# Recurrence's tail moved into the compression, loads reordered, and the routing rebuilt, in a one-core decoder layer

## The chip, the cores and the metric

One of the eight cores of a Trainium2 chip runs the whole kernel. The metric is the device time of one execution in microseconds (us); less is better. Engines: PE (TensorE, matrix products; PEld is its weight load), DVE (VectorE), ACT (ScalarE), POOL (GpSimd), SP (SyncE, which here only issues DMAs). They run side by side and are ordered by semaphores alone.

## The reference, cut to what matters

One layer for a prompt of 256 tokens and 8 samples of one token, which share all weights (264 token columns in all):

```python
h = rms_norm(x)                               # D_MODEL 1024
p = h @ w_in                                  # RWKV-7 columns, NSA columns, two merge gates
y_a = rwkv7(p_a)                              # 8 heads of 64: S = S*w + (S a) b^T + v k^T ; y = S r
                                              # then group norm, bonus, gate
y_b = nsa(p_b)                                # compressed, selected and windowed attention over paged caches
x = x + (sig(g_a) * (y_a @ w_br_a) + sig(g_b) * (y_b @ w_br_b)) @ w_out
h = rms_norm(x)                               # norm_ffn
logits = h @ w_router + b_router              # 32 experts, top 4, softmax over the 4
x = x + sum_k w_k * (swiglu(h @ w_up[e] + b_up[e]) @ w_down[e] + b_down[e])
y = rms_norm(x)
```

The compressed branch of the attention passes each block of 32 cached rows (keys and values apart) through a two-layer network with a gelu, for the samples' 1024 past positions and the prompt's own rows.

## The kernel before, in words

Everything is fp32. The work is a row of blocks; in each, every engine has its own hand-written list of instructions, and a block ends when all engines are through with theirs. A helper `step` (line 132) makes an instruction signal its engine and the engine wait for it; `copy` on ACT has one line in a block.

- **Projection** (`project`, 203): norm, the input projection, and the inputs of the recurrence.
- **Recurrence** (`rwkv_chunks`, 533): the prompt's 256 tokens in chunks of 64. PE, ACT and DVE invert the chunks' triangular matrices in five levels (`t1`, `dxy`; DVE masks the next level at line 675). Beside it POOL advances the 8 samples' states in products of 128x2048 (lines 650 to 658), with two sums on DVE (710, 731); the state goes out, and the samples' y goes through DRAM to be turned by PE (873). The block's tail is the group norm of y: means and variances by PE (879, 882), squares and roots on ACT, reciprocal, product and affine on DVE (739 to 741), bonus and gate on POOL (662, 663). SP also loads the compression's early weights here, and POOL gathers piece 0 of the cache.
- **Compression** (`compress`, 911): 64 units. In unit u PE turns two tiles of gathered rows (1081), ACT (u even) or DVE (u odd) copies them to one of four buffers, and PE multiplies those of unit u-2 with the first layer's weights (1045). Pieces of 1 MB serve 8 units each; three buffers hold them, so piece p is gathered once unit 8(p-2) is turned (`cmp_piece`, 168). At nine units a set-up product uses bank 3 (`at_unit`, `setup`, 1048): three for the table of relative biases (1056), four of the queries, the gates, and 16 small ones for the compressed scores' biases (1069). SP issues page ids, `hot`, the late weights, and then `rel_bias`, which the first set-up waits for along with `hot`.
- **Prompt's attention** (`attend_prompt`, 1102): compressed scores, their softmax on DVE and ACT, turned at line 1100 and copied at 1202; between them PE makes the first merge-gate tiles (1252), whose weights SP loads at the block's start (1130), two buffers deep. Then 16 units of scores (1277), exp, turns and values, with a gate tile in each of the first twelve. POOL issues 16 gathers of selected rows (1147) at the start and the copy of the window cache (1149).
- **Samples' attention** (1319) and **merge** (1559), which at its end adds to x, loaded again.
- **Routing** (`route`, 1651): SP loads six constants (1693), then expert 0's up and down weights, and stores h for the gathers. POOL loads the experts' biases three times over; ACT and DVE split them into three bf16 parts (1719, 1751, 1808), stacked in 96 rows. The norm of x waits for the constants (1749); PE turns h (1828) with ACT's evictions, multiplies with the router (1833). DVE adds the bias (1756), finds the top four, and from ranks by PE (1839, 1841) derives for each token its slot in its expert's 64-row tile; lines 1776 to 1784 list the experts of overflow tiles. PE turns the cells into a table of rows (1846), which DVE reads at 1811. The weights' normalisation ends DVE's list (1817, 1818).
- **Experts** (`first_tiles`): 32 experts. SP streams 8 MB of up and 4 MB of down weights per expert through 16 slots of a ring; a slot is refilled once PE has used it (`up_used`, `down_used`). POOL gathers an expert's rows of h and scatters its results. PE: up products (2016), up bias by a one-hot `pick` in bf16 (2022), turns (1997, 2003), down products (2034), down bias (2039). Overflow tiles (`further_tiles`) aren't run with these inputs.
- **Finish**: the four results of a token are added, and the last norm.

## Time and profile before

| what | us |
|---|---|
| median of 3 runs (lowest, highest) | 1717.59 (1707.12, 1718.58) |
| the profiled execution | 1712.36 |
| its span in the profile | 1710.6 |
| PE busy in the span | 1355.0 (79%) |
| DVE, ACT, POOL busy | 371.0, 223.0, 171.6 |

The profiled execution's time holds its span and 1.8 us around it. "Granted clock" is the share of TensorE's full clock (2.4 GHz) that it was given, 0.50 being the lower level of 1.2 GHz. A releaser (`<-`) behind an idle time is the instruction or DMA that the profile names as the one that ended it. DMA share is the mean busy share of the core's 16 DMA engines.

### The profile page before, as it was taken

The numbers are of one execution on the slowest core, as the hardware profiler recorded it, in microseconds if no ns is written. First come the engines' busy times: TensorE is split into PE (matmuls) and PEld (weight loads), VectorE is DVE, ScalarE is ACT, GpSimd is POOL, SyncE is SP. The second block draws the span as 40 slices with busy tenths as digits, with TensorE's granted clock in tenths as the row PEclk, the third lists the DMA queues.
The fourth block names the chain that finished last, engine by engine and source line by source line (L and its number), as shares of the span: only waits on it lengthen the run. The fifth ranks groups of instructions, "written<-read, shape, count | busy, mean of one in ns | idle before, by whom it ended". The sixth has DMA issues, their size and how long they took to land. (4 is left out here: it accounts for less than half of the span.)

```text
span 1710.6 us, 21148 instructions
## 1 busy us (share of the span) xinstructions
PE 1355.0 (79%) x8102; PEld 690.3 (40%) x8103; DVE 371.0 (22%) x792; ACT 223.0 (13%) x478; POOL 171.6 (10%) x226
## 2 busy tenths in 40 slices
PE   6998838997998945797788887777887887778870
PEld 5878724665877834232222222222222222222220
DVE  3457441122335215111001001010010010100104
ACT  2211120221222023010000000000000000000001
POOL 1004520121000000100000000100001000000010
PEclk9999965898989985799999999999999999999995
DMA  5425133237214446899999999999999999999953
GB/s 173 130 62 120 27 89 106 75 121 297 90 70 129 124 116 254 338 416 415 418 417 415 418 416 417 418 415 418 416 417 418 415 418 416 415 418 415 416 237 141
DMA packets 142944, 489.60 MB, mean 286 GB/s; under 512 B 18958, under 2 KB 67344, under 8 KB 109440
## 3 DMA queue, kind: packets, MB, share of 16 engines
q1 hardware_dynamic: 131848, 457.15, 68.6%
q0 software_dynamic: 10640, 31.11, 5.1%
q8 instruction: 41, 0.67, 0.2%
q10 hardware_dynamic: 400, 0.55, 0.1%
q14 instruction: 15, 0.12, 0.0%
HBM read 484.37 MB, written 16.95 MB: 293 GB/s over the span
## 5 line engine op out<-in xcount | busy, mean ns | idle before, releaser
L2016 PE MATMUL bank<-ex_ring,ex_work 128*64 128x512 f32 x2048 | 515.6, 634 | 170.1 <-DMA ex_ring<-in_w_up 168.3
L2016 PEld LDWEIGHTS bank<-ex_ring,ex_work 128*64 128x64 f32 x2048 | 136.2, 142 | 521.3 <-DMA ex_ring<-in_w_up 299.1
L2034 PE MATMUL bank<-ex_ring,ex_work 128*64 128x512 f32 x1024 | 226.8, 595 | 0.8 <-ACT ex_work L1938 0.8
L1973 DVE TENSOR_SCALAR ex_work<-bank 128x512 f32<-128x512 f32 x32 | 22.1, 692 | 713.6 <-PE bank L2022 713.6
L2034 PEld LDWEIGHTS bank<-ex_ring,ex_work 128*64 128x64 f32 x1024 | 70.7, 137 | 134.1 <-issue 133.1
L1918 POOL DMA_INDIRECT scratch_choice<-ex_work,ex_di x32 | 33.4, 1043 | 665.6 <-ACT ex_work L1948 665.6
L468 PE MATMUL bank<-hT,w_group 128*128 128x264 f32 (+1 forms) x400 | 92.6, 394 | 0.6 <-DVE hT L371 0.6
L468 PEld LDWEIGHTS bank<-hT,w_group 128*128 128x128 f32 (+1 forms) x400 | 76.0, 191 | 16.1 <-issue 0.7
L1252 PE MATMUL bank<-hT,w_cmp 128*128 128x264 f32 x256 | 66.2, 408 | 4.7 <-DMA w_cmp<-in_w_in 4.7
L1938 ACT ACTIVATE ex_work<-bank 128x512 f32<-128x512 f32 x32 | 19.1, 597 | 359.3 <-PE bank L2003 359.3
L1934 ACT ACTIVATE ex_work<-bank 128x512 f32<-128x512 f32 x33 | 19.7, 598 | 344.2 <-PE bank L1997 344.2
L1252 PEld LDWEIGHTS bank<-hT,w_cmp 128*128 128x128 f32 x256 | 49.1, 200 | 15.6 <-DMA w_cmp<-in_w_in 5.2
L1948 ACT ACTIVATE ex_work<-bank 128x512 f32<-128x512 f32 x32 | 19.1, 597 | 202.2 <-PE bank L2039 202.2
L1984 DVE COPY ex_pick_down<-ex_pick 96x64 bf16 x31 | 5.9, 191 | 158.6 <-PE bank L2039 158.6
L1910 POOL DMA_INDIRECT ex_work<-scratch_h,ex_si x33 | 34.6, 1048 | 41.1 <-POOL ex_si L1905 24.3
L1010 DVE COPY pT<-bank 128x256 f32<-128x256 f32 x32 | 13.6, 426 | 101.2 <-PE bank L1081 100.9
L1997 PE MATMUL bank<-masks,ex_work 128*128 128x128 f32 x132 | 22.1, 291 | 12.2 <-DMA ex_work<-scratch_h,ex_si 12.2
L1081 PE MATMUL bank<-masks,x 128*128 128x128 f32 x96 | 18.6, 326 | 14.6 <-PEq L120 14.6
L1618 PE MATMUL bank<-mixed,sel_rows 128*128 128x264 f32 x128 | 28.7, 387 | 1.5 <-DVE mixed L1592 1.5
L1045 PE MATMUL bank<-pT,w_cmp 64*128 64x265 f32 x128 | 29.9, 553 | 0.0
L1618 PEld LDWEIGHTS bank<-mixed,sel_rows 128*128 128x128 f32 x128 | 24.2, 190 | 6.0 <-DVE mixed L1592 1.9
L1905 POOL COPY ex_si<-src_row 128x1 uint32 (+1 forms) x33 | 6.1, 185 | 190.2 <-DMA scratch_choice<-ex_work,ex_di 182.0
(465 smaller groups left out, 1370.1 us busy)
## 6 DMA issues: line engine op xcount, KB each, us to landing
ex_ring<-in_w_up SPq DMA_DIRECT2D x256, 1024.0 KB, 17.9
ex_ring<-in_w_down SPq DMA_DIRECT2D x256, 512.0 KB, 17.2
w_group<-in_w_in SPq DMA_DIRECT2D x12, 1024.0 KB
w_cmp<-in_w_in SPq DMA_DIRECT2D x8, 1024.0 KB, 7.4
sel_rows<-in_w_out SPq DMA_DIRECT2D x8, 512.0 KB, 7.2
choice_rows<-scratch_choice SPq DMA_DIRECT2D x2, 2048.0 KB, 10.4
out_win_s<-in_state_win_kv POOLq DMA_DIRECT2D x1, 4088.0 KB, 26.8
win_rows<-in_state_win_kv SPq DMA_DIRECT2D x6, 512.0 KB
```

The costliest lines, as they stand in the source:

```text
L468: mm = mmul(banks[2 + i % 4][0:n, 0:T], w[:, g % 3, kc, c:c + n], hT[:, kc, :], start=(kc == 0), stop=(kc == KD - 1))
L1045: mmul(banks[4 + 2 * kv + g][:, 0:T + 1], w1[r // 16][gs, kv, r % 16, :], fl[gs, u % 4, :], start=(r == 0), stop=(r == 31)).then_inc(hid, 1)
L1252: mm = mmul(gate_bank(t)[:, 0:T], w[:, t // 2 % 2, kc, P * (t % 2):P * (t % 2) + P], C["hT"][:, kc, :], start=(kc == 0), stop=(kc == KD - 1))
L1618: mm = mmul(banks[m % 2][:, 0:T], sel[:, c, m // 4, m % 4, P:256], mix[:, c, :], start=(c == 0), stop=(c == KD - 1))
L1910: pool.indirect_dma_start(B["xg"][:], None, halves(scratch["h"]), bass.IndirectOffsetOnAxis(ap=B["si"][:, 0:1], axis=0), bounds_check=last ...
L1918: pool.indirect_dma_start(halves(scratch["choice"]), bass.IndirectOffsetOnAxis(ap=B["di"][:, 0:1], axis=0), B["y"][:], None, bounds_check= ...
L1934: nc.scalar.activation(B["xT"][:].rearrange("p a b -> p (a b)"), banks[6][:], ACT.Copy).then_inc(S["xT_ready"], 1)
L1938: nc.scalar.activation(B["hT"][:].rearrange("p a b -> p (a b)"), banks[7][:], ACT.Copy).then_inc(S["hT_ready"], 1)
L1973: nc.vector.tensor_scalar(g[:], banks[0][:], 7.0, None, ALU.min).then_inc(S["g_ready"], 1)
L1997: mm = nc.tensor.transpose(banks[6][:, P * k:P * k + P], B["xg"][:, P * k:P * k + P], ident)
L2016: mm = mmul(banks[n // 2][lo:lo + SLOTS, :], B["xT"][:, k % 4, SLOTS * (k // 4):SLOTS * (k // 4) + SLOTS], B["ring"][:, k, 512 * n:512 * n ...
L2034: mm = mmul(banks[4][SLOTS * n:SLOTS * n + SLOTS, :], B["hT"][:, k % 4, SLOTS * (k // 4):SLOTS * (k // 4) + SLOTS], B["ring"][:, 8 + 4 * h ...
```

## The change

- The samples' part of the recurrence and the whole group norm leave the recurrence's block and become part of the compression. The samples' state is advanced by DVE in 16 tasks of 128x1024 (`sample_half`), one in each odd unit below 32. Eight more set-up products (means and variances) and the turn of the samples' y are placed at units 38 to 56; ACT takes squares and roots, DVE the reciprocals at units 55 to 61, POOL bonus and gate as the norms come. The final state's stores are waited for in the compression.
- The compression has eight piece buffers (in the room of the selected rows), and POOL issues all seven gathers at its start. `rel_bias` is loaded ahead of the late weights. The 16 small bias products go. After unit 31 SP loads the first two groups of gate weights.
- The prompt's attention reads the compressed scores' biases from the bias table in four additions, after a memset by POOL. POOL waits for a gate tile before each pair of gathers of selected rows, and for the twelfth before the window copy.
- Samples' attention: two of the window buffers lie in x. Merge: SP loads the routing's six constants after x.
- Routing: PE turns x itself; DVE evicts with the norm's gain, and the root of the mean square is applied to the logits. The biases are loaded once, in fp32 (32 rows), with no split; the bias products of the experts are fp32. SP loads up weights of expert 0, stores h, then loads the down weights of experts 0 and 1. The list of overflow experts is made by fewer operations behind the comparison (`hit`), which is cut into three parts with a signal each; the weights' normalisation stands ahead of the table's wait.

The diff, cut to its core:

```diff
@@ cmp_piece, gate_weights
-                pool.indirect_dma_start(C["raw"][p % 3][:, t, :], None, src, ...)
+                pool.indirect_dma_start(C["raw"][p][:, t, :], None, src, ...)
+        def gate_weights(sp, g):
+            c0 = 3096 + 256 * g
+            sp.dma_start(C["gate_w"][:, g % 2], a["w_in"][0][:, c0:c0 + 256]...).then_inc(C["gate_in"][g % 2], 16)
@@ rwkv_chunks
-                    tt_(tmp[:], sS[:], keys(kk), ALU.mult).then_inc(prod, 1)
-                    step(tt_(sS[:], sS[:], keys(w), ALU.mult))
...
-                    for m in range(4):
-                        mmul(banks[m][:, 0:T], mean_m, y[:, m, :], start=True, stop=True).then_inc(mean_d, 1)
...
-                    sp.wait_ge(wkv_out, 64)
@@ compress
-                at_unit = [6 + 4 * i for i in range(9)]
-                on_act = (3, 4, 5, 6, 7)
+                at_unit = [4, 8, 12, 16, 18, 20, 22, 26, 38, 40, 42, 44, 46, 50, 52, 54, 56]
+                on_act = (3, 4, 5, 6, 7, 8, 13, 14, 15, 16)
                     sp.dma_start(hot, a["c_hot"]).then_inc(hin, 16)
+                    sp.dma_start(rel[:], a["rel_bias"]).then_inc(hin, 16)
                     cmp_weights(sp, w1[1], 1, w_late)
-                    sp.dma_start(rel[:], a["rel_bias"]).then_inc(hin, 16)
...
+                    sp.wait_ge(hid, 64)
+                    for g in range(2):
+                        gate_weights(sp, g)
...
-                    cmp_piece(pool, 1)
-                    cmp_piece(pool, 2)
-                    for p in range(3, 8):
-                        pool.wait_ge(turned, 8 * (p - 2))
+                    for p in range(1, 8):
                         cmp_piece(pool, p)
...
+                        if u < 32:
+                            if u == 1:
+                                dve.wait_ge(s_in, 16 * 14)
+                            sample_half(u // 2)
+                        if u in (55, 57, 59, 61):
+                            m = (u - 55) // 2
+                            dve.wait_ge(set_a, n_a(14 + m))
+                            step(nc.vector.reciprocal(e[:, m, :], e[:, m, :]))
@@ attend_prompt
-                    for g in range(NG // 2):
-                        if g >= 2:
-                            sp.wait_ge(mtd, 2 * (g - 1))
+                    for g in range(2, NG // 2):
+                        sp.wait_ge(mtd, 2 * (g - 1))
+                        gate_weights(sp, g)
...
                     for s in range(NB):
+                        pool.wait_ge(mtd, s + 1)
...
+                    pool.wait_ge(mtd, 12)
                     pool.dma_start(o["win_s"]...)
@@ route, SP
+                    sp.dma_start(B["bias"][:, 0:2 * FF], a["b_up"][0]).then_inc(b_in, 16)
...
-                    for k in range(8):
-                        sp.dma_start(B["ring"][:, 8 + k // 2, ...], a["w_down"][0][0, P * k:P * k + P, :])...
                     for t, (t0, n) in enumerate(TILES):
                         sp.wait_ge(hg_ok, t + 1)
                         sp.dma_start(scratch["h"][t0:t0 + n, :], h[0:n, t, :]).then_inc(st_, 16)
+                    for e in range(2):
+                        for k in range(8):
+                            sp.dma_start(B["ring"][:, 8 + 4 * e + k // 2, ...], a["w_down"][0][e, P * k:P * k + P, :])...
@@ route, DVE and PE
+                    for k in range(KD):
+                        dve.wait_ge(hTd, k + 1)
+                        ts_(hT[:, k, :], banks[k % 2][:, 0:T], col("norm_ffn", k), None, ALU.mult).then_inc(hTe, 1)
...
-                        step(tt_(lg[0:n, t, :], banks[2 + t][0:n, 0:NEXP], br[0:n, :], ALU.add))
+                        step(stt(lg[0:n, t, :], banks[2 + t][0:n, 0:NEXP], ss[0:n, t:t + 1], br[0:n, :], ALU.mult, ALU.add))
...
-                    pe.wait_ge(hg_ok, 3)
                     for k in range(KD):
...
-                            mm = nc.tensor.transpose(banks[k % 2][:, t0:t0 + n], h[0:n, t, P * k:P * k + P], ident[0:n, 0:n])
+                            mm = nc.tensor.transpose(banks[k % 2][:, t0:t0 + n], x[0:n, t, P * k:P * k + P], ident[0:n, 0:n])
@@ expert_buffers
-            for name, shape, dt in (("ring", [P, 16, 2 * FF], F32), ("bias", [96, 3 * FF], BF16), ("pick", [96, NEXP + 1], BF16),
+            for name, shape, dt in (("ring", [P, 16, 2 * FF], F32), ("bias", [NEXP, 3 * FF], F32), ("pick", [NEXP, NEXP + 1], F32),
```

## Rows read from the trace of the kernel before

**Rows 1.** Windows by stage; columns as in the first line.

```profile
core 0: us, PE busy (x) PEld busy (x) DVE busy (x) ACT busy (x) POOL busy (x), PEclk, DMA share, GB/s
...
150.00:195.00 45.00, 34.97 (x931) 32.93 (x928) 34.17 (x37) 6.46 (x11) 34.59 (x11) 0.89 0.35 74
...
213.30:241.10 27.80, 6.70 (x21) 5.07 (x21) 14.37 (x19) 5.70 (x13) 5.92 (x8) 0.65 0.03 6
...
249.80:262.50 12.70, 0.76 (x6) 0.32 (x6) 0.00 (x0) 0.48 (x2) 0.00 (x0) 0.60 0.99 218
262.50:296.00 33.50, 33.50 (x106) 17.73 (x106) 4.77 (x16) 2.90 (x12) 3.76 (x4) 0.50 0.27 86
296.00:370.00 74.00, 71.76 (x433) 46.72 (x432) 13.20 (x53) 16.69 (x57) 5.65 (x7) 0.93 0.17 55
370.00:405.80 35.80, 26.54 (x129) 21.22 (x129) 6.34 (x20) 2.77 (x5) 19.07 (x34) 0.76 0.95 367
...
622.70:686.40 63.70, 23.85 (x114) 19.82 (x114) 30.83 (x77) 23.95 (x31) 3.49 (x7) 0.51 0.70 249
...
697.10:1665.00 967.90, 797.18 (x3520) 244.98 (x3520) 94.61 (x191) 74.87 (x129) 78.03 (x126) 0.97 1.00 408
```

**Rows 2.** Timeline, recurrence, DVE's masking line and POOL's first product: start, us, instruction.

```profile
147.15 0.69 DVE L675 TENSOR_TENSOR m_level_wu<-m_L,masks 128x512 f32<-128x512 f32 x1
...
153.17 4.56 POOL L650 TENSOR_TENSOR rw_bt_kt<-sample_state,sample_vec 128x2048 f32<-128x2048 f32 x1
...
154.06 4.23 DVE L675 TENSOR_TENSOR m_level_wu<-m_L,masks 128x512 f32<-128x512 f32 x1
```

**Rows 3.** Timeline, end of the recurrence and start of the compression.

```profile
212.60 0.68 PE L869 MATMUL bank<-masks,m_AK 64*64 64x64 f32 x16
...
238.60 0.74 POOL L663 TENSOR_TENSOR yaT<-pT,rw_gate 128x264 f32<-128x264 f32 x1
...
241.10 2.90 PE L1081 MATMUL bank<-masks,x 128*128 128x128 f32 x12 [14.55 <-PEq L120]
```

**Rows 4.** Timeline, compression, PE: bias table and layer-one products.

```profile
262.49 1.87 PE L1056 MATMUL bank<-yb_tok,rel_bias 32*8 32x512 f32 x2 [11.95 <-DMA rel_bias<-in_rel_bias]
...
267.77 1.25 PE L1045 MATMUL bank<-pT,w_cmp 64*128 64x265 f32 x4
...
270.10 1.25 PE L1045 MATMUL bank<-pT,w_cmp 64*128 64x265 f32 x4
...
305.39 0.72 PE L1045 MATMUL bank<-pT,w_cmp 64*128 64x265 f32 x4
...
306.68 0.72 PE L1045 MATMUL bank<-pT,w_cmp 64*128 64x265 f32 x4
```

**Rows 5.** Timeline, start of the prompt's attention, PE.

```profile
398.01 3.58 PE L1100 MATMUL bank<-masks,cmp_p 128*8 128x128 f32 x16 [8.06 <-DVE cmp_pT L1202]
...
405.79 1.57 PE L1277 MATMUL bank<-pT 64*128 64x128 f32 x8
```

**Rows 6.** Timeline, routing, to expert 0's first products.

```profile
641.16 6.63 PE L1828 MATMUL bank<-masks,ex_work 128*128 128x128 f32 x24 [20.41 <-DVE ex_work L1749]
...
648.27 7.99 PE L1833 MATMUL bank<-w_router_sb,h_T 128*128 128x32 f32 x48 [0.48 <-ACT h_T L1725]
...
656.37 0.18 DVE L1756 TENSOR_TENSOR logits<-bank,b_router_sb 8x32 f32<-8x32 f32 x1 [0.24 <-PE bank L1833]
...
665.21 0.68 DVE L1779 TENSOR_TENSOR over_w<-extra_base,numbers 1x512 f32<-1x512 f32 x1
...
675.93 1.76 DVE L1805 TENSOR_TENSOR h_T<-numbers,rt_slot 128x1536 f32<-128x1536 f32 x1
...
697.10 8.26 PE L2016 MATMUL bank<-ex_ring,ex_work 128*64 128x512 f32 x24 [0.69 <-ACT ex_work L1934]
```

**Rows 7.** Timeline, an expert's last K step of up and its biases.

```profile
1025.63 1.94 PE L2016 MATMUL bank<-ex_ring,ex_work 128*64 128x512 f32 x8 [0.57 <-DMA ex_ring<-in_w_up]
...
1027.40 0.60 PE L2022 MATMUL bank<-ex_bias,ex_pick_up 96*64 96x512 bf16 x4
```

More of the change, by code:

```diff
@@ L146, in build @@
         prm = sb(ctx, "prm", [P, NPRM])
+        gain = sb(ctx, "ffn_gain", [P, D])
+        R = {}
+        after = P
+        for name, cols_ in (("wr", KD * NEXP), ("num", 2 * P + 1), ("rk", 2 * P), ("br", NEXP), ("dest", 3 * TOPK * 2)):
+            R[name] = masks[:, after:after + cols_]
+            after += cols_
+        R["wr"], R["rk"] = R["wr"].rearrange("p (c n) -> p c n", n=NEXP), R["rk"].rearrange("p (c n) -> p c n", n=P)
+        R["dest"] = R["dest"].rearrange("p (t k j) -> p t k j", t=3, k=TOPK)
+        R["in"] = sem("route_consts_in", True)
         x = sb(ctx, "x", [P, 3, D])
@@ L191, in rwkv @@
                 ar = sb(st, "rw_at_rt", [P, 2, 4, T])
-                q = {n: sb(st, "rw_" + n, [P, 4, T]) for n in ("gate", "k2")}
+                q = {"gate": C["gate"], "k2": sb(st, "rw_k2", [P, 4, T])}
                 bk = sb(st, "rw_bt_kt", [P, 2, 4, T])
@@ L619, in _ @@
                     act.wait_ge(yd, 1)
-                    copy(y[:, :, P:TP].rearrange("p m (c t) -> p c m t", c=2), banks[5].rearrange("p (c m t) -> p c m t", c=2, m=4)).then_inc(ye, 1)
-                    for m in range(4):
-                        act.wait_ge(cent, m + 1)
-                        nc.scalar.activation(e[:, m, :], y[:, m, :], ACT.Square).then_inc(sqr, 1)
-                    act.wait_ge(eps_ok, 1)
-                    for m in range(4):
-                        act.wait_ge(var_d, m + 1)
-                        nc.scalar.activation(e[:, m, :], banks[4 + m][:, 0:T], ACT.Sqrt, bias=eps[:, 0:1]).then_inc(root, 1)
+                    copy(y[:, :, P:TP].rearrange("p m (c t) -> p c m t", c=2), banks[5].rearrange("p (c m t) -> p c m t", c=2, m=4))
                 @block.gpsimd
@@ L982, in _ @@
                                 nc.scalar.activation(qg[:, i - 3, :], banks[3][:, 0:T], ACT.Copy, scale=SCALE).then_inc(set_a, 1)
+                            elif i == 8:
+                                copy(y[:, :, TP:T], banks[3][:, 0:4 * TS].rearrange("p (m t) -> p m t", m=4)).then_inc(set_a, 1)
+                            elif i >= 13:
+                                act.wait_ge(eps_ok, 1)
+                                nc.scalar.activation(e[:, i - 13, :], banks[3][:, 0:T], ACT.Sqrt, bias=eps[:, 0:1]).then_inc(set_a, 1)
                             else:
@@ L1563, in merge @@
                 oT = sb(st, "outT", [P, KD, T])
-                ta, tb = sb(st, "gated_a", [P, 2, T]), sb(st, "gated_b", [P, 2, T])
+                ta, tb = (C["gate"][:, 2 * i:2 * i + 2, :] for i in range(2))
                 ab, mix_ok, od, oe, td, te = (sem("mg_" + n) for n in
@@ L1733, in _ @@
                                              accum_out=tsum[0:n, t:t + 1]).then_inc(ex, 1)
-                    act.wait_ge(rest_ok, 2)
-                    copy(B["bias"][64:96], rest[64:96])
                 @block.vector
@@ L1762, in _ @@
                     red(asg[:], oh[:].rearrange("p t k e -> p t e k"), axis=AX).then_inc(asg_ok, 1)
+                    for j in range(2):
+                        step(tt_(cell[:, :, :, j, 0:NEXP], oh[:], dest[:, :, :, j].unsqueeze(3).to_broadcast([P, 3, TOPK, NEXP]), ALU.mult))
                     dve.wait_ge(rkd, 1)
```

315 lines of the change are left out of this document (147 added, 168 removed).

## The prediction

> **What bounds the kernel now.** I cut the span into stages with the view by windows [rows 1], then read, stage by stage, the timeline for what the next stage's first instruction had waited for.
>
> The last 1000 us are the 32 experts. From 697.1 to 1665 us the DMA moves 408 GB/s at a share of 1.00, while PE is busy 797 of 968 us [rows 1]: the weights' transfer sets this stage, and PE idles 171/32 = 5.3 us per expert. A product in the stage waits for its weights by half a microsecond at a time [rows 7]. So nothing before the stage helps by making it faster; an edit helps by letting its first product come earlier than 697.10 [rows 6].
>
> In the first 700 us no one engine is full. PE is the busiest, and what is lost lies in places where it stands: 6.7 busy of 27.8 us at the recurrence's end, 0.8 of 12.7 us early in the compression, then 33.5 us of full work at a granted clock of 0.50, 26.5 of 35.8 us at the start of the prompt's attention, 23.9 of 63.7 us in the routing [rows 1]. The change touches each of these.
>
> **Part A, samples' state taken out of the recurrence (150 to 195 us).** POOL's 128x2048 products go. Beside the first, of 4.56 us, DVE's 128x512 masking took 4.23 us; the same line took 0.69 us before POOL began [rows 2]. PE idles 45.0 - 35.0 = 10.0 us in the stretch, with the granted clock at 0.89 [rows 1]. These DVE operations feed the next product of the chain, so most of the idle time is theirs. What stays is the true chain product, copy, product. Bounds: 3 us (only the three worst meetings), 14 us (all idle time and the low clock). I take 9, nearest to the idle time.
>
> **Part B, the recurrence's tail.** PE's last product of the recurrence proper starts at 212.60 and takes 0.68; PE next has steady work at 241.10, 27.8 us on. The last instruction of the tail (POOL, 238.60 + 0.74) ends 1.8 us before that, which is the price of the change of block [rows 3]. Afterwards only the copies of the final state and of y and SP's two stores stand between: by a 128x512 operation of 0.69 us [rows 2] and two DMA issues about 2 us, and 1.8 us for the change: 3.8 us. The final waits for these stores go with the block's last lines. Gain 24; bounds 20 and 26.
>
> **Part C, the compression (241.1 to 370.0 us, 128.9 us).** A unit is one pair of turned rows plus a layer-one product. At full clock units follow each other by 306.68 - 305.39 = 1.29 us, at half clock by 270.10 - 267.77 = 2.33 us [rows 4]. Built up for the changed kernel:
> - 64 units at 1.29 = 82.6 us.
> - 17 set-up products. The bias row took 1.87 us at the low clock [rows 4], 0.95 at the full one; three of these, four head products, eight means and variances (each about as a layer-one product, 0.5 to 0.7 us) and two small ones: 10.6 us. The old kernel's 16 tiny bias products go.
> - the ends: the first turns, then gelu, keys and values as a chain of some ten operations of 0.5 to 0.7 us, which I put at 7 us, as before.
> That is 100 us. Three additions:
> - PE's stall of 11.95 us on the bias table goes [rows 4]: its DMA is now issued ahead of the late weights, and not behind them. I leave 1 to 2 us, since seven gathers of 1 MB are now issued at once (7 MB at 408 GB/s [rows 1] is 17 us, and the 2 MB of late weights beside them). Piece p is needed after 8p units, 10.3p us, so the flood keeps ahead of its readers.
> - DVE gets 16 tasks of 128x1024 in the odd units up to 31. From 0.69 us for 512 columns [rows 2] a task is about 1.3 us, one of them in each half 2.5. DVE's own copies are some 0.6 us of a two-unit period of 2.58, so 1.9 of 2.58 is full, and a copy has more than 1 us of slack because three banks are in use. Cover is there at both clocks. At the end the four reciprocal, product, affine chains (some 2.7 us each beside a copy) come every 2.58 us: that falls behind by 0.7 each and costs PE 2 us.
> - The low clock. 33.5 us at 0.50 followed the stall of 12.7 us [rows 1]. Without the stall I expect shorter stretches, about 18 us in all: 9 us more. Bounds: none, and the whole 44 us as before (20 us).
> The Trainium skill ("TensorE: Matmul & The Clock Gate", section "What's actually happening") has the array back at full clock after a short stretch of sustained work. The row of 262.5 to 296 us disagrees: PE was busy all 33.5 us and the granted clock stayed at 0.50. By the page's rule this stage would end some 9 us earlier than I say; I go by the row.
> Sum 112 us, gain 17; bounds 0 (all of the low clock returns, with flood stalls) and 27.
>
> **Part D, the prompt's attention up to its first scores (370.0 to 405.8 us, 35.8 us).** The gate weights' first two loads move into the compression, and the 16 gathers of the selected rows wait for one gate product each. Now the DMA is saturated here (share 0.95, 367 GB/s [rows 1]), PE stands for 8.06 us before the second turning of the compressed probabilities, and the first scores come at 405.79 [rows 5]. In all PE idles 35.8 - 26.5 = 9.3 us with a granted clock of 0.76 [rows 1]. With gate weights at hand and the DMA not full, about 1 us of the idle time stays and 2 us of the low clock goes: 26 us. The bias is now added in four operations in place of eight, with cover under the gates. Queued behind POOL's new waits is only its own window copy, which lands long before 504 us. That copy now starts after the twelfth gate and meets the last gate load: 0 to 3 us. Gain 10; bounds 0 and 12.
>
> The samples' attention changes only places of buffers: nothing. The merge gains six DMAs on SP, behind the loads that PE waits for and none ahead of them: nothing, since the merge's own products cover them. Without that cover they would cost the routing what they cost now.
>
> **Part E, routing (622.7 to 697.1 us).** Two things hold the first turn until 641.16: the wait for the constants' DMAs and the norm's products behind it (PE's 20.41 us of waiting [rows 6]). Afterwards x is turned at once, at 622.8. Eight turns with an eviction each, 6.6 us as now [rows 6], end at 629.4; the 48 router products, 7.99 us, at 637.4. Meanwhile DVE does the norm's three 128x1024 products (from rows 2 about 4 us) after its last eviction and is free at 634.5. So the last logit addition, now at 656.37, comes at 637.5: 18.9 us. From there to the table: five of the over-list's operations of 0.68 and two or three small ones leave the path (4.0 us), one 0.6 us product goes, 0.2 is added: 4.4 us. The 1.76 us comparison goes in three parts, and PE begins after the first: 1.2 us. The weights' normalisation (six small operations of 0.2, as the one at 656.37) leaves the tail: 1.3 us. Sum 25.8 us, so routing ends near 661 in place of 686.4 and expert 0's first product stands near 671, the gather's 10.7 us (686.4 to 697.10 [rows 1, 6]) kept. The bias parts on ACT and DVE go altogether. Bounds 18 and 29 (with the array at full clock right behind the merge, where the row has 0.51).
> Who is late next: SP now issues 8.4 MB of up and 8.4 MB of down weights, at 408 GB/s done near 666. That is before 671, but the first gather's rows travel with them, as they do now; and expert 1's down weights, which now are loaded in this gap, are no longer to be loaded there.
>
> **Part F, biases in fp32.** The four bias products of up took 0.60 us in bf16; one K step of the same shape in fp32 takes 1.94 [rows 7]. So +1.3 for up, +0.6 for down, 1.9 us per expert against 5.3 idle: hidden for 31 experts. Past the last transfer nothing hides it: two down biases and one up bias, +2.5 us. Upper bound per expert: about 6 us, if the products don't pair.
>
> **Sum.** 9 + 24 + 17 + 10 + 25.8 - 2.5 = 83.3 us. Against the profiled execution, 1712.36 us (its span 1710.6): 1629. The median of the runs is 1717.59, 5.2 above it, so I predict 1634.
>
> **Rivals.**
> 1. The compression stays at half clock although it isn't stalled. For: the row 262.5 to 296. Against: 296 to 370 us, the same work, has 0.93 [rows 1]. Price: in 40 us of low clock 18 us in place of 9, 1643; for all 64 units 64 x 1.04 = 67, less 9: 1692.
> 2. The flood: gathers, late weights and DVE's tasks stall the compression as the saturated DMA does in part D, by 8 to 20 us: 1642 to 1654. For: 8.06 us of stall under 367 GB/s [rows 5]. Against: work waits here for 1 MB per 10 us only.
> 3. Routing's end falls to SP's queue or to the first gather behind 17 MB of weights: 5 to 8 us late, 1641.
> 4. The other side: PE overtakes the DMA as the experts' bound. One mechanism: 1.9 us more per expert at a long low clock. At full clock it has room (24.9 + 1.9 against 30.2 us). At half clock an expert takes 53.6 against 30.2, 23 us lost for each. It decides once four experts in a row run so: 83/23. Eight would give 1634 + 187 = 1821. Against: clock 0.97 over the stage [rows 1], and more work on PE doesn't call for a lower one.
> 5. More than forecast: full clock in the compression and the routing, 1615.
>
> **How the numbers follow.** Forecast 0.58, rival 1 0.12, rival 2 0.12, rival 3 0.07, rival 4 0.03, rival 5 0.08. Predicted is the likeliest, 1634. The range 1610 to 1668 takes in rivals 2, 3 and 5, and rival 1 but for its worst. A measurement of this kernel can tell about 1%, 17 us. Faster by over 1%: 0.95; within: 0.02; slower: 0.03 (rival 4).
>
> **What would show each step.** In the changed profile: DVE's masking line at 0.69 us throughout (A); some 4 us from the recurrence's last product to the compression's first (B); no wait on the bias table, a stage of about 112 us and its granted clock (C); 26 us to the first scores (D); from the merge's end to the first expert product about 49 us where there were 74 (E); the experts' stage again near 968 us at 408 GB/s (F). If that stage is longer by more than 10 us, or the compression over 125 us, the prediction is wrong.

## Result and profile after

| | before | changed |
|---|---|---|
| median of 4 runs (lowest, highest), us | 1718.09 (1707.12, 1720.77) | 1628.15 (1623.85, 1631.19) |
| profiled execution (span), us | 1712.36 (1710.6) | 1623.85 (1622.0) |
| PE busy, mean granted clock of the experts' stage | 1355.0, 0.97 | 1371.4, 1.00 |

The changed kernel takes 0.953 of the time of before [0.948, 0.957], 5% less. Forecast were 1634 us and a range of 1610 to 1668. Profile against profile 88.5 us are gained; the sum of the forecast was 83.3. Executions of one kernel fall into two states some per cent apart, and every ratio in this document compares fast executions with fast ones, so it can differ from the ratio of two medians.

The view by windows, cut at the first instructions of the same stages as in [rows 1]; columns as there:

```profile
core 0: us, PE busy (x) PEld busy (x) DVE busy (x) ACT busy (x) POOL busy (x), PEclk, DMA share, GB/s
150.00:204.45 54.45, 47.78 (x1401) 45.64 (x1401) 27.07 (x48) 8.68 (x14) 3.16 (x4) 1.00 0.20 43
204.45:208.71 4.26, 0.68 (x17) 0.57 (x17) 0.80 (x3) 1.04 (x3) 0.00 (x0) 0.97 0.20 35
208.71:309.86 101.15, 96.19 (x574) 61.01 (x574) 54.66 (x120) 27.27 (x89) 22.44 (x23) 0.96 0.49 144
309.86:336.77 26.91, 26.91 (x128) 22.46 (x129) 5.76 (x16) 2.77 (x5) 9.19 (x24) 0.79 0.45 153
336.77:437.52 100.75, 92.37 (x482) 78.15 (x481) 35.24 (x112) 27.16 (x93) 10.10 (x11) 0.91 0.43 154
...
551.96:603.36 51.40, 25.41 (x127) 20.72 (x127) 29.33 (x89) 7.73 (x18) 2.01 (x4) 0.55 0.91 358
603.36:1573.10 969.74, 843.55 (x3712) 247.55 (x3712) 94.03 (x191) 74.62 (x128) 77.87 (x126) 1.00 0.99 407
1573.10:1622.00 48.90, 0.04 (x2) 0.00 (x0) 19.68 (x21) 5.71 (x11) 0.99 (x1) 0.54 0.35 126
```

The timeline of the changed kernel at those places (start, us, instruction, idle time before it and its releaser):

```profile
154.37 0.69 DVE L644 TENSOR_TENSOR m_level_wu<-m_L,masks 128x512 f32<-128x512 f32 x1
...
204.45 0.68 PE L825 MATMUL bank<-masks,m_AK 64*64 64x64 f32 x16
208.71 2.90 PE L1102 MATMUL bank<-masks,x 128*128 128x128 f32 x12 [3.58 <-PEq L120]
...
215.50 1.02 PE L1073 MATMUL bank<-yb_tok,rel_bias 32*8 32x512 f32 x2
...
309.86 6.14 PE L1268 MATMUL bank<-KcT,pT 64*128 64x8 f32 x32 [1.01 <-PEq L857]
...
336.77 1.57 PE L1302 MATMUL bank<-pT 64*128 64x128 f32 x8
...
405.32 3.89 PE L1277 MATMUL bank<-hT,w_cmp 128*128 128x264 f32 x8 [4.47 <-DMA w_cmp<-in_w_in]
...
561.74 7.99 PE L1829 MATMUL bank<-masks,h_T 128*128 128x32 f32 x48 [0.59 <-DVE h_T L1745]
...
603.36 3.68 PE L2012 MATMUL bank<-ex_ring,ex_work 128*64 128x512 f32 x8 [0.69 <-ACT ex_work L1930]
...
1553.23 1.93 PE L2018 MATMUL bank<-ex_bias,ex_pick_up 32*64 32x512 f32 x8
```

Read against the rows of before:

| stretch | before | changed | gain | forecast |
|---|---|---|---|---|
| A: to the recurrence's last product (L869, now L825) | 212.60 | 204.45 | 8.2 | 9 |
| B: from there to the compression's first turn | 28.50 | 4.26 | 24.2 | 24 |
| C: compression, to the attention's first product | 128.92 | 101.15 | 27.8 | 17 |
| D: from there to the first scores | 35.77 | 26.91 | 8.9 | 10 |
| first scores to samples' attention | 98.73 | 100.75 | -2.0 | 0 to -3 |
| samples' attention and merge, to its last product | 115.04 | 114.44 | 0.6 | 0 |
| E: merge's last product to expert 0's first | 77.54 | 51.40 | 26.1 | 25.8 |
| F: experts' stage | 967.6 | 969.8 | -2.2 | 0 |
| F: last product to the end | 45.9 | 48.9 | -3.0 | -2.5 (both F rows) |

Four of the rows come out within 1 us. The one large gap is C, and most of it is the clock: PE turns its first pair at 208.71, meets the bias table at 215.50 without a wait, and from 217 us up to the end of the 64 units, near 299 us, the granted clock is 1.00, where before had 33.5 us at 0.50 [rows 1, 4]. The gap is 10.8 us; 9 of it is the low clock that the forecast kept, the rest the small waits that it allowed for and that did not come. The experts' stage moves 407 GB/s, as before; the bias products (L2018, 1.93 us) stand where PE would have waited.

### The profile page after: what moved, and what is told of

Read it like the earlier page. It is cut to its first block and busy times, and to the rows that moved or that the text cites. A ratio compares the mean times of both kernels' runs of the same rounds, so it can differ in the third digit from the quotient of the medians.

```text
span 1622.0 us, 21473 instructions
## 1 busy us (share of the span) xinstructions
PE 1371.4 (85%) x8262; PEld 674.8 (42%) x8263; DVE 372.4 (23%) x810; ACT 206.1 (13%) x464; POOL 139.5 (9%) x213
## 5 line engine op out<-in xcount | busy, mean ns | idle before, releaser
L2012 PE MATMUL bank<-ex_ring,ex_work 128*64 128x512 f32 x2048 | 492.0, 606 | 125.9 <-DMA ex_ring<-in_w_up 124.4
L2012 PEld LDWEIGHTS bank<-ex_ring,ex_work 128*64 128x64 f32 x2048 | 128.8, 136 | 465.6 <-DMA ex_ring<-in_w_up 280.4
L2030 PE MATMUL bank<-ex_ring,ex_work 128*64 128x512 f32 x1024 | 226.8, 596 | 0.7 <-ACT ex_work L1934 0.7
L2030 PEld LDWEIGHTS bank<-ex_ring,ex_work 128*64 128x64 f32 x1024 | 70.7, 137 | 134.0 <-issue 133.1
L2018 PE MATMUL bank<-ex_bias,ex_pick_up 32*64 32x512 f32 x256 | 61.8, 600 | 0.0
L1277 PEld LDWEIGHTS bank<-hT,w_cmp 128*128 128x128 f32 x256 | 49.6, 202 | 15.3 <-DMA w_cmp<-in_w_in 5.2
L1980 DVE COPY ex_pick_down<-ex_pick 32x64 f32 x31 | 5.6, 182 | 183.0 <-PE bank L2035 183.0
L2035 PE MATMUL bank<-ex_bias,ex_pick_down 32*64 32x512 f32 x128 | 34.4, 613 | 0.0
L2018 PEld LDWEIGHTS bank<-ex_bias,ex_pick_up 32*64 32x64 f32 x256 | 15.0, 131 | 44.6 <-issue 44.6
L1102 PE MATMUL bank<-masks,sel_rows 128*128 128x128 f32 x192 | 33.3, 296 | 0.0
L1102 PEld LDWEIGHTS bank<-masks,sel_rows 128*128 128x128 f32 x192 | 25.7, 190 | 13.9 <-issue 4.4
```

What stands on the lines that cost most here:

```text
L1102: mm = mmul(banks[u % 3][:, P * t:P * t + P], raw[p][:, t, c0:c0 + P], ident, start=True, stop=True)
L1277: mm = mmul(gate_bank(t)[:, 0:T], w[:, t // 2 % 2, kc, P * (t % 2):P * (t % 2) + P], C["hT"][:, kc, :], start=(kc == 0), stop=(kc == KD - 1))
L2012: mm = mmul(banks[n // 2][lo:lo + SLOTS, :], B["xT"][:, k % 4, SLOTS * (k // 4):SLOTS * (k // 4) + SLOTS], B["ring"][:, k, 512 * n:512 * n ...
L2018: mm = mmul(banks[n // 2][lo:lo + SLOTS, :], B["pick_up"][:], B["bias"][:, 512 * n:512 * n + 512], start=False, stop=True)
L2030: mm = mmul(banks[4][SLOTS * n:SLOTS * n + SLOTS, :], B["hT"][:, k % 4, SLOTS * (k // 4):SLOTS * (k // 4) + SLOTS], B["ring"][:, 8 + 4 * h ...
L2035: mm = mmul(banks[4][SLOTS * n:SLOTS * n + SLOTS, :], B["pick_down"][:], B["bias"][:, 2 * FF + 512 * n:2 * FF + 512 * n + 512], start=Fals ...
```

## Experiments

Stage times of all versions, from their timelines, in us (C, D, E as above; "units" is the first scores to the samples' attention). Absolute medians of different groups come from different chips, so the ratio to before is the safer number. Only single executions stand behind before_again and pool_products; stage times are always those of one profiled execution. Stages that no edit touched agree within 1.5 us, but for the compression of three versions, told below, and for "units", which takes 98.7 and 104.4 us in the two profiles of the kernel before, and 100.4 to 103.8 in those changed kernels that have the same instructions there, so differences below 4 us in that column say little.

| version | median | ratio to before, 95% | C | D | units | E | experts | end |
|---|---|---|---|---|---|---|---|---|
| before | 1718.1 | 1 | 128.9 | 35.8 | 98.7 | 77.5 | 967.6 | 45.9 |
| changed | 1628.2 | 0.948-0.957 | 101.2 | 26.9 | 100.8 | 51.4 | 969.8 | 48.9 |
| before_again | 1716.8 | | 131.3 | 35.7 | 104.4 | 76.4 | 967.6 | 46.2 |
| b_table_first | 1693.5 | 0.985-0.994 | 110.9 | 27.2 | 112.7 | 77.2 | 967.4 | 47.6 |
| table_late | 1666.7 | 0.970-0.983 | 144.4 | 26.3 | 100.4 | 51.4 | 970.6 | 49.5 |
| sel_unpaced | 1634.7 | 0.956-0.966 | 101.1 | 27.0 | 107.9 | 51.4 | 970.8 | 48.9 |
| gates_late | 1626.7 | 0.948-0.959 | 101.1 | 27.0 | 100.9 | 51.5 | 970.7 | 49.7 |
| both_undone | 1651.4 | 0.954-0.967 | 116.2 | 36.7 | 100.4 | 51.5 | 970.5 | 48.9 |
| route_back | 1643.8 | 0.953-0.964 | 108.2 | 27.0 | 100.9 | 61.0 | 970.8 | 48.5 |
| win_early | 1626.8 | 0.944-0.954 | 110.5 | 25.8 | 97.2 | 51.2 | 970.3 | 49.6 |
| win_paced | 1621.5 | 0.948-0.959 | 102.1 | 26.2 | 96.8 | 51.3 | 971.1 | 48.9 |
| pool_products | 1638.5 | | 101.5 | 27.0 | 103.3 | 51.2 | 970.4 | 49.8 |
| bias_x2 | 1636.0 | 0.953-0.969 | 101.1 | 27.4 | 103.8 | 51.3 | 974.7 | 49.7 |
| bias_x3 | 1826.7 | 1.065-1.082 | 101.0 | 27.4 | 100.8 | 51.3 | 1171.7 | 49.6 |

**The bias table and the clock (part C).** In the kernel before, the table goes ahead; in the changed one, back behind the late weights:

```diff
+ sp.dma_start(rel[:], a["rel_bias"]).then_inc(hin, 16)
  cmp_weights(sp, w1[1], 1, w_late)
- sp.dma_start(rel[:], a["rel_bias"]).then_inc(hin, 16)
```

> The kernel before, with the table of relative biases loaded ahead of the late weights and nothing else changed. The recurrence's idle tail of 28 us stays, the stall of 11.95 us on the table should go. The compression (its first turn to the attention's first product) takes 128.9 us before. If the stall called down the low clock behind it (33.5 us at 0.50, worth 16.8 us), the stage takes 100 us and shows no long stretch at 0.50: the time falls by some 29 us. If the idle tail ahead of the stage had called it down, it stays wherever the stall is gone: 117 us, 12 us faster. My forecast's reckoning, half of the low clock stays: 109 us.

> The changed kernel, with the table loaded behind the late weights again, as before. Now there is a stall but no idle tail ahead of it. The compression takes 101.2 us in the changed kernel. Stall alone: the table comes behind 2 MB of late weights that share the queues with 7 MB of gathers, so the stall is 12 to 20 us; if nothing follows it, the stage takes 113 to 121 us. If a stall calls down some 34 us at 0.50, another 17 us are lost: 130 to 138 us, and the kernel gives back 29 to 37 us of its gain from this one line.

table_late, windows of its compression, and the product that waits:

```profile
218.80:245.47 26.67, 0.01 (x2) 0.01 (x1) 1.95 (x2) 0.00 (x0) 8.86 (x9) 0.58 1.01 313
245.47:278.00 32.53, 32.53 (x102) 17.45 (x102) 11.47 (x22) 2.90 (x12) 0.00 (x0) 0.50 0.13 37
```

```profile
245.47 1.87 PE L1073 MATMUL bank<-yb_tok,rel_bias 32*8 32x512 f32 x2 [26.66 <-DMA rel_bias<-in_rel_bias]
```

The stall is 26.66 us, longer than expected, and behind it PE is busy for 32.5 us at a granted clock of 0.50. The stage grows by 43.2 us: 26.7 of stall, and 32.5/2 = 16.3 of clock. There is no idle tail ahead of it, so a stall inside the stage is enough to call down the low clock, and the 33.5 us of [rows 1] are most likely the same thing. Why it lasts so long isn't shown: after the 8.06 us before the compressed probabilities' second turning in the kernel before [rows 5] it is back at 1.00 by 402.6, 4.6 us on.

b_table_first gave neither 29 nor 12 us; its compression is 18.0 us shorter. Its windows, and the set-up product at which the clock falls:

```profile
245.00:295.00 50.00, 50.00 (x307) 29.86 (x305) 10.38 (x39) 11.38 (x42) 7.58 (x9) 1.00 0.72 188
295.00:298.00 3.00, 3.00 (x26) 2.65 (x26) 0.00 (x0) 0.48 (x2) 0.00 (x0) 0.98 0.01 3
298.00:328.00 30.00, 30.00 (x108) 19.52 (x107) 3.21 (x13) 2.90 (x12) 1.87 (x2) 0.50 0.11 36
328.00:350.80 22.80, 20.55 (x132) 13.04 (x129) 4.95 (x20) 5.78 (x17) 0.02 (x1) 0.95 0.00 1
```

```profile
294.90 0.72 PE L1045 MATMUL bank<-pT,w_cmp_late 64*128 64x265 f32 x4
295.55 4.66 PE L1069 MATMUL bank<-rel_bias,yb_tok 32*128 32x8 f32 x31
```

The 11.95 us of stall are gone and the clock is 1.00 for 50 us, in spite of the idle tail ahead of the stage. Then it falls at 298 us, with no idle time at all: PE is in the small bias products of eight columns (L1069), the ones that the change deletes, and 30 us follow at 0.50. The kernel before has the same, shorter:

```profile
324.24 4.05 PE L1069 MATMUL bank<-rel_bias,yb_tok 32*128 32x8 f32 x32
```

```profile
324.00:328.00 4.00, 4.00 (x36) 3.76 (x32) 0.00 (x0) 0.18 (x2) 0.00 (x0) 0.94 0.01 2
328.00:336.00 8.00, 8.00 (x29) 5.27 (x29) 1.20 (x5) 0.48 (x2) 1.88 (x2) 0.50 0.41 131
```

So the old compression had two low stretches, one behind the stall and one that begins inside these products. The change takes away the stall and the products, and its 64 units run at 1.00. For the stall table_late shows it by itself. For the products it is read from where the clock falls (in both profiles of the kernel before and in b_table_first); no run takes them away alone. My reckoning, half stays, hit the size of this run (109) but not its reason.

**The attention's start (part D).**

```diff
  for s in range(NB):
-     pool.wait_ge(mtd, s + 1)
```

```diff
- for g in range(2):
-     gate_weights(sp, g)
...
- for g in range(2, NG // 2):
-     sp.wait_ge(mtd, 2 * (g - 1))
+ for g in range(NG // 2):
+     if g >= 2:
+         sp.wait_ge(mtd, 2 * (g - 1))
      gate_weights(sp, g)
```

The first is sel_unpaced, the second gates_late (its first lines stood in the compression).

> The changed kernel without POOL's waits for a gate tile before each pair of gathers of selected rows: all 16 are issued at once. If the full DMA was what stalled PE for 8.06 us before the first scores, the stretch from the attention's first product to its first scores takes some 33 us (26.9 now). If the gate weights' early load alone took the stall away, it stays at 27 us, within 1 us.

> The changed kernel with the first two groups of gate weights loaded at the attention's start, as before; the gathers of selected rows stay paced by the gates. Those weights land some 8 us after the issue. If the early load matters, PE waits for them 3 to 6 us after the compressed scores (which take 6 us), and a low clock behind adds 2 to 4: 32 to 36 us to the first scores in place of 26.9. If pacing alone did it, 27 to 29 us.

Both stay at 27.0 us. Unpaced gathers only move the cost: PE waits 3.45 us for gate weights at 341.77 (timeline of sel_unpaced), and its units take 7.1 us more. So I undid both at once (both_undone), and profiled the kernel before a second time.

> The changed kernel with both edits of part D undone: gate weights loaded at the attention's start, all 16 gathers of selected rows issued at once. Each alone left the stretch from the attention's first product to its first scores at 27.0 us. If the 8.06 us stall of before needs both at once, the stretch takes 33 to 36 us now. If it came from something else in the kernel before, or from chance, it stays at 27 us, and the gain of part D isn't the change's.

> The kernel before, unchanged, for a second profile. If the stall of 8.06 us ahead of the compressed probabilities' second turning belongs to the kernel, it stands there again and the stretch to the first scores takes 35.8 us. If it belongs to one execution, the stretch takes some 27 us. The stall of 11.95 us on the bias table and the low clock behind it, some 33 us long, should stand there in either case.

both_undone, timeline of PE and DVE; the idle time and its releaser stand last:

```profile
346.68 0.27 PE L1118 MATMUL bank<-masks,cmp_p 128*8 128x128 f32 x1 [0.42 <-issue]
353.99 3.58 PE L1118 MATMUL bank<-masks,cmp_p 128*8 128x128 f32 x16 [7.04 <-DVE cmp_pT L1225]
...
353.25 1.28 DVE L1225 COPY cmp_pT<-bank 8x512 f32<-8x512 f32 x2 [12.55 <-remote]
```

The stall is back, 7.04 us, and D is 36.7; before_again has it too, 8.27 us. So it belongs to the program and not to one execution, and in the changed kernel it comes back only when both edits are undone; either edit alone brings the 27 us. But late gate weights and a full DMA together are not enough for it. b_table_first has neither edit and got through D in 27.2 us with PE never idle:

```profile
350.82:378.06 27.24, 27.24 (x129) 22.63 (x129) 6.43 (x20) 2.77 (x5) 18.95 (x34) 0.78 0.98 375
```

It paid later: PE waited 10.32 us for a gate's weights at 404 us, and its units took 112.7. What the stall waits for stays open, and with it how much of D's gain the two edits as such have brought. In both_undone PE stands for DVE's copy, and DVE starts it 6 us after PE's last product, though it waits for nothing else that this block computes: the profile writes "remote", which names no engine and no load.

**A like stall in the compression.** both_undone, route_back and win_early have their edits elsewhere, and yet their compression takes 108 to 116 us.

> The changed kernel with the copy of the window cache (4 MB read and written, 24.8 us) issued in the recurrence, once the early weights have landed, where the DMA moves 3 to 9 GB/s for 35 us. It no longer meets the last gate weights, for which PE waits 4.47 us at 405 us and then makes a gate tile at half clock, 1.9 us. Forecast: from the first scores to the samples' attention 94 us in place of 100.7, and the kernel 5 to 7 us faster. Rival: the copy is still under way when the compression gathers its pieces, or holds up the stores of the state, and costs there what it saves: same within 2 us.

```diff
+ pool.wait_ge(C["w_in"], 96)
+ pool.dma_start(o["win_s"]...).then_inc(win_copied, 16)
...
- pool.wait_ge(mtd, 12)
- pool.dma_start(o["win_s"]...).then_inc(win_copied, 16)
```

The forecast for the attention held in half: no wait on the last gate weights, D and units together 4.6 us shorter (units 97.2 us where I had written 94). But the compression lost 9.3 us, and the kernel is not shown to be faster than the changed one (ratios 0.949 and 0.953, with overlapping intervals), where I had written 5 to 7 us. win_early, timeline of PE and ACT there, and its windows:

```profile
223.79 0.72 PE L1065 MATMUL bank<-sel_rows,w_cmp 64*128 64x265 f32 x4 [2.81 <-issue]
...
228.28 1.25 PE L1065 MATMUL bank<-sel_rows,w_cmp 64*128 64x265 f32 x4 [1.57 <-issue]
...
223.25 0.38 ACT L939 ACTIVATE sel_rows<-bank 128x256 f32<-128x256 f32 x1 [8.08 <-remote]
...
229.19 0.38 ACT L939 ACTIVATE sel_rows<-bank 128x256 f32<-128x256 f32 x1 [5.45 <-remote]
```

```profile
219.00:229.00 10.00, 5.19 (x24) 2.64 (x22) 3.53 (x7) 0.48 (x2) 6.24 (x7) 0.81 1.04 353
229.00:250.00 21.00, 21.00 (x115) 12.33 (x111) 13.03 (x26) 4.54 (x17) 0.00 (x0) 0.85 0.82 248
```

ACT stands for 8.08 and 5.45 us and PE for 2.81 and 1.57 us with no engine or load as releaser, under a DMA share of 1.04; a low clock follows, though a short one. The copy is not under way any more by then: it was issued near 162 us and takes 24.4. The DMA view shows the queue that brings the engines' code: in the changed kernel it moves a packet between 224 and 228 us; in the three versions that stall, none between 206 and 232, and the next between 232 and 236, when they go on. I took this for code that comes late behind seven gathers of 1 MB. The times don't bear it out: ACT's last stand ends at 229.19 in win_early, and the packet comes only after 232, so the packet may be late because the engines were. win_paced is the same kernel, with pieces 3 to 7 paced.

```diff
  for p in range(1, 8):
+     if p >= 3:
+         pool.wait_ge(turned, 8 * (p - 2))
      cmp_piece(pool, p)
```

> The changed kernel with the early window copy and one edit more: in the compression, pieces 3 to 7 are gathered once unit 8(p-2) is turned, as before the change, in place of all seven at once. With the early copy alone the compression took 110.5 us against 101.2 in the changed kernel, though nothing in it had been edited: PE, DVE and ACT stood together for 3 to 8 us between 219 and 229 us without a releaser that one of them owed, under a DMA share of 1.04. If these stands come from the full DMA (the engines' code comes by the same DMA engines), pacing takes them away: 101 to 103 us, and the kernel is 8 to 10 us faster than with the early copy alone, near 1617 us. If they come from where the code lies, or from the copy in the recurrence, they stay: 108 to 112 us, and no gain.

win_paced, windows, and the changed kernel's window over the same times:

```profile
219.00:229.00 10.00, 10.00 (x58) 5.56 (x59) 6.25 (x13) 1.45 (x6) 1.96 (x2) 1.00 1.09 282
```

```profile
219.00:229.00 10.00, 10.00 (x60) 5.77 (x60) 6.27 (x11) 1.45 (x6) 8.17 (x7) 1.00 1.04 346
```

PE is busy all 10 us, at the full clock, and the compression is back at 102.1. That does not show the cause. The changed kernel has the same DMA share of 1.04 in these 10 us, and win_paced an even higher one, and PE is busy throughout in both, so a full DMA does not bring the stall by itself. Nor is pacing shown to cure it: six versions with all seven gathers at once (changed, sel_unpaced, gates_late, pool_products, bias_x2, bias_x3) don't stall either, at 101.0 to 101.5 us, and any edit, this one too, also moves the code that follows. Whether a version stalls differs between programs that are the same in this stage; why is open. win_paced is 5.3 us below win_early in the median, less than the 8 to 10 expected, and not at all in the ratio to before (0.953 against 0.949). Against the changed kernel it is 6.6 us lower in the median with the same ratio, 0.953: its profile is shorter (expert 0 starts at 598.72 against 603.36), but the times do not settle that it is faster.

**Routing (part E).**

```diff
- for k in range(KD):
-     dve.wait_ge(hTd, k + 1)
-     ts_(hT[:, k, :], banks[k % 2][:, 0:T], col("norm_ffn", k), None, ALU.mult).then_inc(hTe, 1)
...
      stt(h[0:n, t, :], x[0:n, t, :], ss[0:n, t:t + 1], gain[0:n, :], ALU.mult, ALU.mult).then_inc(hg_ok, 1)
+ for k in range(KD):
+     dve.wait_ge(hTd, k + 1)
+     ts_(hT[:, k, :], banks[k % 2][:, 0:T], col("norm_ffn", k), None, ALU.mult).then_inc(hTe, 1)
...
- for t in range(3):
-     tt_(hit[:, t], ...).then_inc(cell_ok, 1)
+ tt_(wl[:], ...)
...
+ tt_(hit[:].rearrange("p a b c -> p (a b) c"), ...).then_inc(cell_ok, 3)
```

> The changed kernel with two parts of the routing undone: DVE makes the norm of x before it evicts the turned tiles, and the list of overflow experts, the comparison in one piece and the weights' normalisation stand again where they stood. From the norm's rows the last eviction comes 8.9 us later; the list costs 1.7, the single piece 1.3, the normalisation 1.2. From the merge's last product to expert 0's first product 64.5 us in place of 51.4. If the weights' stream had been what the first expert waits for, the end moves less than this stretch: it would be seen as an experts' stage that is shorter by the difference. By my reckoning the stream is through by then, and the whole kernel is 13 us slower than the changed one.

The two kernels' rows, counted from the merge's last product (551.96 changed, 560.41 here): the router begins 9.8 and 18.4 us after it (8.6 for the norm's place), the table's product 34.3 and 45.9 (another 3.0 for list and comparison), the routing's list on DVE ends at 41.1 and 54.0 (1.3 for the normalisation, put behind the table). Sum 12.9; 13.1 was expected. But expert 0 begins only 9.6 us later. route_back's first gather and the turn that waits for it, and then the changed kernel's:

```profile
616.69 1.10 POOL L1905 DMA_INDIRECT ex_work<-scratch_h,ex_si  x1 [0.83 <-POOL ex_si L1900]
...
619.64 1.12 PE L1992 MATMUL bank<-masks,ex_work 128*128 128x128 f32 x4 [7.66 <-DMA ex_work<-scratch_h,ex_si]
```

```profile
595.37 1.10 POOL L1906 DMA_INDIRECT ex_work<-scratch_h,ex_si  x1 [0.83 <-POOL ex_si L1901]
...
601.55 1.12 PE L1993 MATMUL bank<-masks,ex_work 128*128 128x128 f32 x4 [9.60 <-DMA ex_work<-scratch_h,ex_si]
```

From the gather's issue to the turn it is 2.95 us here and 6.18 us in the changed kernel, where the weights are still on their way (the DMA moves 408 GB/s from 590 to 602 us). A faster routing now meets the weights' stream; 3.2 us of the 12.9 were hidden by that. The median is 15.6 us above the changed kernel's; the profile puts 9.6 of it here and 7.1 into the compression told above.

**POOL beside DVE (part A).** Fourteen products were added to the recurrence:

```diff
+ pool.wait_ge(s_in, 16 * 14)
+ for i in range(14):
+     step(tt_(junk, sS[:, 16 * (i % 2):16 * (i % 2) + 16], vec[:, 0][:, None, :].to_broadcast([P, 16, HD]), ALU.mult))
```

> The changed kernel with 14 extra products of 128x1024 on POOL in the recurrence, whose results nobody reads: the size of the products that the change took out, without their sums on DVE. If POOL's products are what held up DVE's maskings, the masking line shows durations of 2 to 4 us beside them in place of 0.69 (its sources are both in SBUF), while the additions that read a bank stay at 0.69, and the recurrence ends 6 to 9 us later. If DVE's own two sums and the larger loads were the cost, it ends within 2 us of the changed kernel's.

pool_products, timeline of the recurrence on DVE and POOL:

```profile
154.69 2.02 DVE L648 TENSOR_TENSOR m_level_wu<-m_L,masks 128x512 f32<-128x512 f32 x1
157.10 0.69 DVE L676 TENSOR_TENSOR m_X<-m_X,bank 128x512 f32<-128x512 f32 x1 [0.39 <-PE bank L743]
...
158.43 8.29 DVE L680 SCALAR_TENSOR_TENSOR pT<-shifted,prm,rw_k 128x264 f32<-128x264 f32 x4
166.63 2.83 DVE L648 TENSOR_TENSOR m_level_wu<-m_L,masks 128x512 f32<-128x512 f32 x1
...
153.80 36.21 POOL L638 TENSOR_TENSOR pT<-pT 128x1024 f32<-128x1024 f32 x14
```

The masking takes 2.02 and 2.83 us in place of 0.69, the four bonus products 8.29 in place of 1.70 (L676 of the changed kernel), all of them with both sources in SBUF; the addition that reads a bank keeps its 0.69. DVE's last copy of the recurrence stands at 214.16 in place of 204.44, 9.4 us later if the 0.3 us by which the first maskings differ are taken off; the granted clock over 150 to 187 falls from 1.00 to 0.82. So POOL's products alone, without the sums on DVE, cost what part A gained (8.2 us), though this is one execution, and the added products are not the same as those taken out.

The Trainium skill ("SBUF — State Buffer", section "SBUF: two separate sides") says that VectorE and GpSimd lock one shared port pair, VectorE when it has two SBUF inputs; the rows of both kinds of operation agree.

**Biases (part F).** The bias products of the experts are issued two and three times, so the biases count double and threefold:

```diff
+ for z in range(3):
      mm = mmul(..., B["pick_up"][:], B["bias"]..., start=False, stop=(z == 2))
```

> The changed kernel with every bias product of the experts done twice (so the biases count double). PE idles 3.9 us per expert in the experts' stage, 126 of 970 us; the second set costs 3.0 us per expert. If the weights' transfer sets the stage, as forecast, it hides all but the last: the stage within 2 us of 970, and up to 4 us more at the end. If PE's idle time is not usable (it lies in front of single K steps of a ring with one expert's room), part of the 96 us shows: 20 us or more.

> The changed kernel with every bias product of the experts done three times. The two extra sets cost 6.0 us per expert against 3.9 idle: PE passes the transfer as the bound, 2.1 us per expert, 66 us over the stage: 1036 to 1040 us in place of 970. If the stage stays below 990, the idle time is larger than the profile shows; if it is above 1060, the two bounds add up before they meet.

bias_x2's stage is 5.0 us longer than the changed kernel's (I had expected at most 2), at a clock of 0.96 in place of 1.00 and DMA share 0.99: 91 of 96 us are hidden. bias_x3 is far off what I expected: 202 us longer in place of 66. Its timeline for one expert, and windows over it:

```profile
1041.21 7.09 PE L2012 MATMUL bank<-ex_ring,ex_work 128*64 128x512 f32 x32
1048.23 7.63 PE L2019 MATMUL bank<-ex_bias,ex_pick_up 32*64 32x512 f32 x24
...
1056.83 8.55 PE L2031 MATMUL bank<-ex_ring,ex_work 128*64 128x512 f32 x32
1065.32 3.70 PE L2037 MATMUL bank<-ex_bias,ex_pick_down 32*64 32x512 f32 x12
```

```profile
1041.00:1048.00 7.00, 7.00 (x35) 2.25 (x33) 0.00 (x0) 0.60 (x1) 0.00 (x0) 1.00 1.02 413
1048.00:1053.00 5.00, 5.00 (x23) 1.96 (x22) 0.00 (x0) 0.00 (x0) 0.00 (x0) 1.00 1.00 421
1053.00:1060.00 7.00, 7.00 (x18) 2.17 (x16) 2.76 (x5) 1.12 (x2) 0.00 (x0) 0.51 0.69 290
1060.00:1065.00 5.00, 5.00 (x26) 1.54 (x22) 0.00 (x0) 0.00 (x0) 0.00 (x0) 1.00 0.70 245
```

All of the time is PE's (busy 1170.3 of 1171.7 us), at a mean granted clock of 0.87. At full clock its work is 843.6 + 2 x 96.2 = 1036 us, the figure that I had expected; the rest, 134 us, is the clock. It falls each time inside or right behind a set of bias products (32 rows in place of the 128 of the products around them), with PE busy throughout: here 4.8 us into the 24 products of up, and stays at 0.50 for some 7 us. Single sets of 1.93 us, as the change has them, leave it at 1.00.

## Why the prediction was right, and where not

- **A, B, E** came out at 8.2, 24.2 and 26.1 us against 9, 24 and 25.8. pool_products confirms A's mechanism. B was not tried alone; it rests on the two traces, where the tail of 28.5 us is gone and 4.26 us stand in its place. Within E the last logit addition comes 18.9 us earlier relative to the merge's end, the very term (36.8 to 17.9), and route_back confirms the terms of the list, comparison and normalisation, 4.2 us of which it undid. What I had as kept, the gather of 10.7 us, has 3.2 us in it that the weights' stream causes.
- **C** was mis-sized: 27.8 against 17, and 0.8 above the upper bound that I had written. The build-up at full clock (100 us) was right to 1 us. The term that failed is "the low clock: 9 us more". I had kept half of the row of 262.5 to 296 as if it belonged to the work itself. table_late shows such a stretch as the sequel of a stall, and the second stretch at 0.50, from 328 us, begins in small products which the change deletes; in the changed kernel the 64 units have neither. The Trainium skill ("TensorE: Matmul & The Clock Gate", section "What's actually happening") would have had this stage 9 us shorter than I said, and for the changed kernel that came true; for the 32.5 us of full work at 0.50 in table_late its account does not hold, nor, as I read it, for a fall under a busy PE as in b_table_first.
- **D** had the right size (8.9 against 10), but its reason isn't shown. I had put the stall down to the full DMA and the late gate weights; both_undone agrees, and b_table_first, which has both and no stall, does not. That the size came out is in part luck. After the window copy in its new place PE waits 4.47 us at 405.32, more than the 0 to 3 that I gave it; the units took 2.0 more than before, which is less than the two profiles of the kernel before differ by.
- **F**: 2.0 us per expert is what the profile shows against 1.9 (61.8 + 34.4 us over 32 experts, less 19.3 + 12.4 for the bf16 products), and it is hidden but for 2.2 us. PE's busy time in the stage grew by 46 us only, from 797.2 to 843.6, because the granted clock also rose, from 0.97 to 1.00. The end took 3.0 us more; it isn't the biases: after the last scatter 14 us pass to the loading of the choices, where there were 11, and every version of the changed kernel has it. Its cause wasn't tried.
- **Rival 1** (half clock without a stall) did not happen here; **rival 2** (the flood) didn't either in this kernel, but three close relatives have a stall there, at 7 to 15 us where I had priced 8 to 20; that the flood is its cause isn't shown. **Rival 3**: 3 us of it are in E. **Rival 4** did not happen; its argument against, "more work on PE doesn't call for a lower one", is refuted by bias_x3: two more sets of biases bring it about, at 134 us of low clock out of 202. **Rival 5** was half true: full clock in the compression, but 0.55 over the routing's stretch, where [rows 1] have 0.51.

The total was right within 6 us, and part of that is luck: C gained 10.8 us more than forecast, and half of it was met by rows that came out lower, each by a little (A, D, the units, F).

## What to carry to other kernels

A stall of PE can cost more than its length: 12 and 27 us of waiting took 16 more behind them, so price a removed wait with its low clock, and look for what else stands where the clock falls (here products of eight columns) before you keep half of it. Not every wait costs that much (behind 8.06 us there were 4.6 us at half clock, some 2 more), so read it from the windows. Before you name a full DMA as the cause of a stall, look for a window with the same share and no stall; here there was one in both stages. A DMA-bound stage hides extra work of PE up to its idle time (here 91 of 96 us), but check what that work does to the clock near the limit.

## What the hardware showed that I had not expected

- The granted clock fell with PE busy without a gap, in or right behind two kinds of runs: 4 us of products of 32 rows by 8 columns (before, b_table_first), and 8 us of products of 32 rows by 512 columns (bias_x3). It was back after 3 to 31 us. What in these products calls for it isn't shown.
- ACT stood for 5 to 8 us, and PE for up to 3 us with it, with no engine or load as releaser, under a DMA share of 1.04; other programs whose instructions there are the same, at the same share, don't. In the attention's start the kernel before stalled in both of its profiles (8.06 and 8.27 us).
- A gather of the same rows lands 2.95 us or 6.18 us after its issue, without or with the weights' stream.
